# One overlapping DMA in place of eight for the Toeplitz block of every eight S5 groups

## The reference, cut to what matters

```python
# x_t = Ab x_{t-1} + Bb u_t ;  y_t = Re(C x_t), for every one of the 128 groups
bu_re = jnp.einsum('bcgh,gph->bcgp', u_i, bb_re)
bu_im = jnp.einsum('bcgh,gph->bcgp', u_i, bb_im)
...
y = jnp.einsum('bcgp,ghp->bcgh', x_r, c_re) - jnp.einsum('bcgp,ghp->bcgh', x_i, c_im)
...
y = y.reshape(b_, l_, SEQ_WIDTH) + d.astype(jnp.float32) * uf
y = jax.nn.gelu(y).astype(h.dtype)
```

## Time and profile before

| what | us |
|---|---|
| median of 3 runs | 4088.63 |
| the profiled execution | 4099.38 |
| its span, first to last instruction | 4097.8 |
| PE busy in it | 3412.5 (83%) |
| DVE busy | 1361.5 (33%) |
| POOL busy | 941.7 (23%) |
| ACT busy | 857.4 (21%) |
| POOL issuing the 128 DMAs on L1097 | 67.9 |
| `S5Outputs`, from POOL's first load to the first product with the gate's weights | 1464.15 to 1646.27 |

### The profile page before, as it was taken

One profiled execution on the slowest core, in us unless ns is written; L12 is line 12 of the kernel. 1 busy time (PEld: TensorE's weight loads), 2 busy tenths in 40 slices (PEclk: granted clock), 3 DMA queues, 4 the chain that ended last, 5 costly groups with the idle time before them and its releaser, 6 DMA issues.

```text
span 4097.8 us, 47269 instructions
## 1 busy us (share of the span) xinstructions
PE 3412.5 (83%) x18042; PEld 2643.9 (65%) x18042; DVE 1361.5 (33%) x2265; ACT 857.4 (21%) x1396; POOL 941.7 (23%) x658
## 2 busy tenths in 40 slices
PE   7997966799977965998985887899999855589998
PEld 4444734567656455445784785699988633369997
DVE  5672024310021720013135554350512333535151
ACT  2112222122121102101224111222222122222221
POOL 0221400333222044003340000044433400004442
PEclk9998966799997955999997996899999955599999
DMA  5981200124366256222220000122222100012222
GB/s 165 253 263 43 93 5 0 47 80 131 118 83 197 74 153 164 69 75 71 87 73 20 1 1 1 46 82 88 82 72 79 52 0 0 6 46 82 88 82 72
DMA packets 112552, 322.26 MB, mean 79 GB/s; under 512 B 35472, under 2 KB 36112, under 8 KB 112160
## 3 DMA queue, kind: packets, MB, share of 16 engines
q1 hardware_dynamic: 59040, 212.89, 16.1%
q0 software_dynamic: 31168, 95.17, 8.9%
q10 hardware_dynamic: 22208, 12.26, 1.1%
HBM read 288.38 MB, written 31.85 MB: 78 GB/s over the span
## 4 chain that ended last, share of the span: by engine, by line
PE 74%; DVE 14%; issue 4%; ACT 3%; POOL 2%; DMA 2%; DVEq 0%; ACTq 0%; POOLq 0%
PE ps L228 15%; PE ps L220 12%; PE ps L223 12%; PE ps L225 11%; PE ps L406 2%; DVE inv L415 2%; PE ps L1837 2%; DVE h L423 2%; POOL ring_r L337 1%; PE ps L250 1%; PE ps L1866 1%; PE ps L244 1%; PE ps L248 1%; PE ps L247 1%; DMA arena<-d_pb 1%
## 5 line engine op out<-in xcount | busy, mean ns | idle before, releaser
L337 POOL TENSOR_TENSOR ring_r<-ring,high 128x1024 fp32r<-128x1024 f32 x274 | 700.3, 2556 | 2152.5 <-ACT high L264 2152.5
L220 PE MATMUL ps<-h_hi,high 128*128 128x264 f32 (+1 forms) x1888 | 553.3, 309 | 61.3 <-DVE h_r L428 39.8
L223 PE MATMUL ps<-h_r,high 128*128 128x264 f32 (+1 forms) x1888 | 548.0, 307 | 0.0
L225 PE MATMUL ps<-h_hi,ring_r 128*128 128x264 f32 (+1 forms) x1888 | 448.7, 305 | 0.0
L264 ACT ACTIVATE high<-ring 128x1024 fp32r<-128x1024 f32 x274 | 289.6, 1057 | 709.5 <-PE ps L220 586.7
L220 PEld LDWEIGHTS ps<-h_hi,high 128*128 128x128 f32 x1888 | 361.3, 191 | 86.3 <-issue 59.4
L228 PE MATMUL ps<-arena,ring 128*128 128x512 f32 (+1 forms) x1024 | 340.1, 496 | 52.6 <-ACT arena L1168 36.1
L223 PEld LDWEIGHTS ps<-h_r,high 128*128 128x128 f32 x1888 | 363.3, 192 | 13.4
L228 PE MATMUL ps<-h,ring 128*128 128x512 f32 x768 | 330.4, 592 | 3.8 <-ACT arena L2161 2.3
L228 PEld LDWEIGHTS ps<-arena,ring 128*128 128x128 f32 x1024 | 197.4, 193 | 195.0 <-issue 141.3
L225 PEld LDWEIGHTS ps<-h_hi,ring_r 128*128 128x128 f32 x1888 | 307.9, 191 | 14.5
(11 more groups left out here) (375 smaller groups left out, 5035.2 us busy)
## 6 DMA issues: line engine op xcount, KB each, us to landing
ring<-in_units SPq DMA_DIRECT2D x402, 512.0 KB, 3.3
arena<-d_ca POOLq DMA_DIRECT2D x32, 640.0 KB, 4.9
d_ca<-arena POOLq DMA_DIRECT2D x16, 640.0 KB, 5.6
arena<-in_s_bk POOLq DMA_DIRECT2D x16, 512.0 KB, 9.1
arena<-d_q POOLq DMA_DIRECT2D x32, 256.0 KB, 11.7
d_pb<-arena POOLq DMA_DIRECT2D x16, 512.0 KB, 6.5
arena<-d_pb POOLq DMA_DIRECT2D x16, 512.0 KB, 5.6
arena<-d_k POOLq DMA_DIRECT2D x128, 64.0 KB, 4.6
```

What stands on the lines that cost most here:

```text
L220: part = mm(acc, hi[:, cols], self.x_hi(k)[:, t0:t0 + tn], start=(k == 0), stop=False)
L223: mm(acc, hi[:, cols], self.x(k)[:, t0:t0 + tn], start=False, stop=False)
L225: ins = mm(acc, w[:, cols], self.x_hi(k)[:, t0:t0 + tn], start=False, stop=(k == self.kt - 1))
L337: b.nc.gpsimd.tensor_tensor(b.ring_r[:, slot, :], b.ring[:, slot, :], self.high[:, j % 2, :], ALU.subtract).then_inc(b.unit_lo, 1)
```

## The change

The eight DMAs of 16 partitions become one DMA of 128 partitions. Its source is written as an access pattern by hand: eight shifts with a step of 16 floats, 16 rows with a step of 1920 floats, eight groups with a step of 240 floats, and 128 floats in a row. The destination is all of `toep`. The same bytes are read from the same addresses and land at the same places, in the same runs of 512 bytes. The DMA that loads `ca` still goes ahead of it. A DMA adds 16 to its semaphore when it has landed, so PE now waits for 32 a block and not for 144.

```diff
         def load(m_, par):
             pool.dma_start(m.ca[par], b.d_ca[m_]).then_inc(self.block_in[par], 16)
-            for k in range(S5_C):
-                pool.dma_start(m.toep[par][16 * k:16 * k + 16], b.d_k[m_][:, :, 16 * k:16 * k + P]
-                               ).then_inc(self.block_in[par], 16)
+            k = b.d_k[m_]
+            shifts = bass.AP(k.tensor, k.offset, [[S5_H, S5_C], [8 * 240, S5_H], [240, 8], [1, P]])
+            pool.dma_start(m.toep[par], shifts).then_inc(self.block_in[par], 16)
...
-            pe.wait_ge(self.block_in[par], it * (16 * 9) + 16 * 9)
+            pe.wait_ge(self.block_in[par], it * 32 + 32)
```

## The result

The kernel before ran in 4088.63 us (median of five runs, 4079.53 to 4093.43), the changed one in 4107.97 us (median of five, 4101.75 to 4120.70). The ratio is 1.0052, with an interval of 1.0029 to 1.0076. The forecast was 4112.0 us. The profiled execution took 4120.70 us with a span of 4119.1, where before had 4099.38 and 4097.8: 21.3 us more.

A forecast was written before the change was run, and what follows sets the result against it. It took the buffer's load loop to bound the stage, closely followed by the DMA engines. Eight engines at 10.3 us a block add 21.0 us, the first block 2.4: 4088.6 + 23.4 = 4112.0 us, range 4084 to 4130.

The forecast's parts named there:

- the likeliest case: toep load: always the same eight engines, 10.3 us of work per block, +23.4 us, 4112.0 us; chance 0.55.
- How many engines: New toep DMA: eight of sixteen engines were taken to carry it, so toep takes 6.0 us and not 3.0.
- The same eight, or by turns: Successive toep loads: the same eight engines each time were taken, read from a steady half rate in other loads.
- the sign of alternating halves: toep transfers: their rate would go up to 174 GB/s when two loads overlap.
- The rival with alternating halves: toep loads switch engine halves from DMA to DMA; intervals of 10.0 us, +19 us, some 4107 us; chance 0.20.
- The loop of a buffer: From POOL's load issue to PE's start two blocks later: 12.4 us in place of 9.9, an interval of 10.0 us.
- The first block: Start of the stage: ca's 4.2 us plus toep's 6.0 make 10.2 us where 7.8 were needed, +2.4 us.
- The clock: Granted clock in the changed stage: the sum took it to give nothing back.
- The rate: toep's 512-byte runs: 174 GB/s on sixteen engines, kept per engine, so 512 KB take 3.0 us of sixteen engines.
- All sixteen, and the issue time won: PE's wait for d_k: sixteen engines carry the load, 4 to 22 us faster, put at -13, 4076 us; chance 0.13.
- POOL's queue: POOL's issue of the new DMA stalls for room in its descriptor queue, could add tens of us; chance 0.02.
- nothing shows: toep load on eight engines overlaps with ca; an interval grows by 0.15 us, 4093 us; chance 0.10.

The follow-up runs named there:

- e9: Changed kernel with four outermost in the load's source pattern and 256 shifts, so other values arrive; 4150.08 us in one run.
- e1: Changed kernel with sixteen outermost in the load's source pattern in place of eight, so other values arrive; 4084.53 us, 0.9966 of the kernel before.
- e2: Changed kernel with the load split into two DMAs, each with eight outermost, and d_k stored to suit; 4089.03 us, 0.9981 of the kernel before.
- e7: Changed kernel plus a small DMA per load, 128 partitions of 64 bytes to SBUF, eight outermost; 4111.90 us, 1.0039 of the kernel before.
- e4: Changed kernel plus a small copy within HBM behind each load, 16 rows of 64 bytes; 4111.66 us, 1.0040 of the kernel before.
- e11: Kernel before, its eight toep DMAs reading plain rows of another array in place of shifted 512-byte runs; 4093.65 us in one run.
- e10: Changed kernel with the shifts made when ACT stores d_k, so the load reads 128 plain 4 KB rows; 4081.30 us, 0.9960 of the kernel before.
- e3: Changed kernel plus a small copy within HBM behind each load, 8 rows of 64 bytes; 4119.53 us, 1.0063 of the kernel before.
- e8: Changed kernel plus a small DMA per load, 128 partitions of 64 bytes to SBUF, sixteen outermost; 4113.35 us in one run.

## Why the prediction was right, and where it wasn't

**Direction and size.** 4112.0 us were forecast against 4107.97, and a stage 23.4 us longer against 16.6. The time in the profiled execution rose by 21.3, of which 4.7 lie outside the changed stage, so the closeness of the sums is partly luck: the term that the change explains was forecast 6.8 us too large. The time couldn't have told the likeliest case from its rival either, since their forecasts, 4112 and 4107 us, lie 5 us apart.

**How many engines.** Eight, as taken: a share of 0.42 to 0.49 with one load, and 0.25 and about 1 for four and sixteen outermost (e9, e1). In the trace of before the half rate of rows 11 stood for eight, and the share there stood against it. The eight DMAs joined to one made the stage 10.2 us shorter in e1 and 16.6 longer in the change itself: joining paid only where the new pattern kept all engines.

**The same eight, or by turns.** This step failed. The likeliest case had the same eight each time, 10.3 us of engine work an interval. The halves alternate: all engines were busy while two loads overlapped, up to 12 us after the first issue, at rates around the 174 GB/s that the forecast named as the sign of alternating halves, and e2 and e7 confirm it. The rival with alternating halves gave a stage 19 us longer and some 4107 us, and that is what came, but I had given it a chance of 0.20, and the fixed eight 0.55. The misstep was in the reading of rows 11, where I trusted the rate against the share: the busy share was right. Even so, the fixed half itself was over-priced. e7 has it, and its interval is 9.55 us, not 10.3. By the forecast's own terms (7.3 us of work for sixteen engines, 3.0 of them `toep`) that leaves `toep` 9.55 - 4.3 = 5.2 us of its eight engines, an estimate, where 6.0 were taken.

**The loop of a buffer.** In that rival the forecast had 12.4 us from POOL's issue to PE's start and an interval of 10.0 from the second block on, after a first one of 7.9. Measured were 12.0 (the mean of the seven loads in the chain) and 9.8 (1489.82 to 1627.26, 14 intervals), after a first one of 6.9; the 9.62 of the table is the mean of all 15. The engines' share is 1.02 and 1.05 in the same stretches. Both bounds have come together here, and I can't tell which ends last. PE's waits for `d_k` without the first were forecast over 45 us and were 38.3: a miss, on the side of the likeliest case's 10.3 us an interval.

**The first block.** Forecast +2.4, measured +3.3 us. Part of it is the issue, which took 1.33 us where 0.77 were taken and 1.03 was the upper bound; so POOL was done 1.9 us after it began, outside the 1.5 that the forecast gave. The landing of 10.7 us at the median was forecast at 10. The last piece of the first block before lands 0.13 us ahead of PE's product at 1471.96:

```profile
1468.40 3.43 DMA arena<-d_k
```

After, the one DMA lands 0.14 us ahead of the product at 1482.95, so the lower count of the semaphore shows neither a gain nor a cost.

**The clock.** It gave nothing back, as the sum took it: the granted clock is 0.50 from POOL's first issue to the gate's product in both kernels, with PE busy for 71 to 73% (1520 to 1600) where it was 77 to 86%. It is 0.50 in e9 as well, with longer gaps (PE busy for 18.57 of 40 us):

```profile
1520.00:1560.00 40.00, 18.57 (x85) 18.03 (x85) 2.25 (x3) 1.79 (x3) 11.31 (x12) 0.50 0.86 156
```

**The rate.** The 174 GB/s held over from rows 9 were the rate of eight small pieces. In one DMA on sixteen engines, e1 moved 0.28 and 0.22 MB of `toep` in one us each. On eight engines one load alone moved 0.08 and 0.11 MB in one us (after) and 115 GB/s at best (e7), with which 524,288 B take 4.6 us. So the term "3.0 us on sixteen, 6.0 on eight" was on the large side, though not in every stretch: at e4's 82 GB/s the load would take 6.4 us.

**All sixteen, and the issue time won.** The rival on the other side was sized at -13 us for sixteen engines; e1 is that case and its stage is 10.2 us shorter, its time 10.3. Its mechanism holds: e11 shows that the short runs explain 0.26 us of before's interval, and e1 that issuing once takes off 0.79 although the runs stay short. The small instructions that the forecast counted between the issues are in the trace of before, for the 80 of the 128 issues that stand in POOL's loop:

```profile
L1097 POOLq FUSED_REGOPS  x80: 37/37/43, 1512.7 to 1597.3; - x80
L1097 POOLq MOVE arena<-d_k x80: 29/29/29, 1512.8 to 1597.3; - x80
```

In the changed kernel there are 10 of each on L1098, of 43 and 29 ns. What they are for is not shown.

**POOL's queue, and nothing shows.** No stall on the new issue appeared; POOL issued each in 1.33 us. That the wait of 38.60 us was one for room in a queue was my supposition: the trace names no releaser for it. The interval grew by 0.88, not 0.15.

## What to carry to other kernels

Before joining DMAs, look at the outermost dimension of the joined pattern: the share of busy engines in a stretch where it moves alone, times sixteen, tells how many engines carry it (about 1 in e1, 0.42 to 0.49 after, 0.25 in e9), and eight of them cost more here than eight issues on POOL had (a stage of 198.7 us against 182.1). Reorder the pattern so that sixteen is outermost (171.9 us in e1), or issue two of eight (172.9 in e2), or, better, pay for an awkward gather once at the store, where most of it was hidden, so that the load reads plain rows (157.3 in e10). When a rate and a busy share contradict each other, find a case that separates them before choosing one.

## What the runs showed that I had not expected

- **The issue time followed the size of the outermost dimension, not only the number of runs.** With 1024 runs of 512 bytes it is 0.90 us for sixteen engines, 1.33 for eight, 2.13 for four (e1, after, e9); 128 plain rows take 0.53 (e10), and the 2048 runs of L956 take 1.03.
- **DMAs of eight engines took the halves by turns here**: the share was 0.96 to 1.13 with two loads in flight (after, 1476 to 1484). A small one of 128 partitions with eight outermost took a turn as well (0.45 to 0.57 in e7, 1475 to 1481); a copy of 8 rows within HBM didn't (0.97 to 1.10 in e3).
- **A fixed half cost no more than taking turns.** With both loads on the same eight engines (e7) the stage is 198.3 us, with turns 198.7 (after) and 199.9 (e8). Alone on eight engines 512-byte runs moved at 82 (e4) to 115 GB/s (e7), on four at 57 (e9), with two loads in flight on all sixteen at 162 to 187 (after). What slows them when two are in flight is open.
- **A busy engine is not a fast one.** The share in the steady stretches rose from 0.76 to 1.02 while the rate fell from 203 to 198 GB/s (1520 to 1560, rows 5 and after).
